# Second FFN of a two-layer trunk: the fourth unit product split in two, its first half ahead of the norm of half 1

## The chip, the cores and the metric

The kernel runs on one core of a Trainium2 chip (trn2). TensorE (PE) multiplies, VectorE (DVE), ScalarE (ACT) and GpSimd (POOL) do the elementwise work, SyncE (SP) issues the transfers. The metric is the device time of one execution in microseconds (us). The kernel before takes 2104.82 us, the median of 3 runs (2103.49 to 2105.01).

## The reference

A trunk of two layers over 1024 latent tokens of 1024 channels with a context of 256 tokens. Layer 0 mixes with a bidirectional gated recurrence, layer 1 with 2-D window means. Each layer then has a gated convolutional feed-forward part (FFN), which is what the change touches in layer 1:

```python
def _conv_ffn(h, w_up, conv_w, conv_b, w_down):
    z = h @ w_up.astype(h.dtype)
    u, v = z[..., :D_FF], z[..., D_FF:]          # D_FF = 3072
    u = _dwconv(u, conv_w, conv_b, (FFN_CONV // 2, FFN_CONV // 2))   # width 3, over positions
    return (jax.nn.gelu(u) * v) @ w_down.astype(h.dtype)

    # in each layer, mod(h) = h * (1 + scale) + shift
    x = x + g_m * _rms_norm(y_lat, norm_post_mix[i])
    f_lat = _conv_ffn(_modulate(_rms_norm(x, norm_pre_ffn[i]), sh_f, sc_f), ...)
    x = x + g_f * _rms_norm(f_lat, norm_post_ffn[i])
```

All data are float32. The kernel gets near-float32 products out of three passes in a rounded type: each operand is split into a rounded part (`_hi`) and the remainder (`_lo`), and a product is hi x hi + hi x lo + lo x hi.

## The kernel before, in words

**Layout.** Channels lie on the 128 partitions in 8 tiles (k = 0 to 7), positions along the free axis in two halves of 512, half 0 and half 1 (`hs(h)`). `H_hi` and `H_lo` hold the normed and modulated input of the FFN. A weight tile of 128x1024 comes by DMA into a raw buffer (`rawA`, `rawB`, `rawC`), ACT rounds it into `W?_hi`, POOL subtracts and writes `W?_lo`.

**The FFN** goes in steps j = 0 to 23 of 128 hidden channels. Steps 0 and 1 compute their u and v directly, and each is a "unit product": 8 tiles k x 3 passes x 2 halves = 48 matmuls of 512 columns. Slot A makes u of step 0, slot B makes v of step 0, slot C (`extra`) makes u of step 1, and slot A a second time makes v of step 1; this is the fourth unit product. From step 2 on the up projection is made by a block scheme of seven quarter products (names 11, 12, S1 to S4, 22) from sums of weight blocks that POOL forms (`combine`) in `So_raw` and in `rawB`; ACT rounds these into `So_hi`, POOL writes the remainder into `So_lo`. `So_lo` and `So_raw` are one and the same memory. After each step `down` multiplies the gated product (`F_hi`, `F_lo`) with the down weights (`WC_hi`, `WC_lo`) into 8 output tiles; in step 0 ACT copies these out of PSUM (`copy_down`), in later steps DVE adds them.

**Ahead of the second FFN.** `first_pair(L, h)` is the function that runs the unit products on half h. On half 0 of layer 1 it runs A and B by turns, then C. Then comes the norm of half 1 (`norm(6, 1)`): three groups of column sums of squares (`square_sums`, 4 matmuls of 1 column each, shown as x8 in the trace), the root on ACT, the reciprocal on DVE, and `spread`, which lays the result over the partitions by four small matmuls. Then `first_pair(1, 1)` on half 1, then the fourth product on both halves, then `down(1, 0)` and the first block step.

**What sets the order.** Each engine has its program in the order in which it is written, and semaphores tie them together. Names that matter here: `w_ready["A"]` says that a slot's weight is split; `unit_done["A"]` that a product of slot A is through; `made` that a block sum stands; `d_copied` that ACT has emptied a tile of `down`. POOL's program at the start of the second FFN (`ffn_first`) is `WA_lo` for the fourth product, block sums S1 and S2 (`So_raw`), `F_lo` of step 0, `WC_lo` of step 0, block sums S3 and S4, and then remainders for the first block step. ACT makes the rounded halves of S4 and S1 ahead of its first `copy_down`, and `down` stops ahead of its fourth tile until that copy is done.

Of the kernel before, what the change touches and what calls it, by code (L numbers as in the profile page):

```python
# [19 lines left out]
P = 128  # L20
# [54 lines left out]
def build_trunk(nc, xT, ctxT, params, ada, wA, wB, wC, gatew, poolw, poolcnt, ident_in, outT):  # L75
    with ExitStack() as top:
# [101 lines left out]
        def nth(order, name, t):  # L178

            return len(order) * t + (order.index(name) + 1 - len(order))  # L180
# [3 lines left out]

        def ready_at(name, t, first=False):
            return nth(READY_FIRST if first else READY_ORDER, name, t)

        def unit_at(s, L, j=0):

# [153 lines left out]
        def evens_to(q, h):  # L343
            each = {"tree": 3, "late": 2, "acc": 0, "pool": 0}
            return sum(chain_end(n, h) - 1 if form(n, h) == "chain" else each[form(n, h)] for n in range(q))
# [236 lines left out]
        def _(pe):  # L582
# [60 lines left out]
                if last:  # L643
                    mm.then_inc(ssq_done[h], 1)

            def square_sums(q, h):

                last, total = square_slot(q, h, KT - 1), square_slot(q, h, 0)
                kind = form(q, h)
                if kind == "chain":  # L650
                    end = chain_end(q, h)
                    if q % 2 == 0:
                        for p in range(end, KT):
                            pe.wait_ge(sq_made[h], 8 * q + p + 1)
                            column_sums(q, h, *square_slot(q, h, p), p == end, False)
                    pe.wait_ge(sum_even[h], evens_to(q + 1, h))
                    column_sums(q, h, *total, q == 1 or end == KT, q != 1 or end == KT)
                    if q == 1 and end < KT:
                        pe.wait_ge(sq_made[h], 8 * q + KT)
                        column_sums(q, h, *last, False, True)  # L660
                elif kind == "late":
                    for n in range(4):
                        if n < 2:
                            pe.wait_ge((sum_even, sum_odd)[n][h], (evens_to, odds_to)[n](q + 1, h))
                        else:
                            pe.wait_ge(sq_made[h], 8 * q + n + 5)
                        column_sums(q, h, *square_slot(q, h, n if n < 2 else n + 4), n == 0, n == 3)
                elif kind == "pool":
                    pe.wait_ge(sum_odd[h], odds_to(q + 1, h))
                    column_sums(q, h, *total, True, True)  # L670
                elif kind == "tree":
                    pe.wait_ge(sum_last[h], trees_to(q + 1, h))
                    column_sums(q, h, *total, True, True)
                else:
                    pe.wait_ge(acc_copied, 1)
                    column_sums(q, h, *total, True, True)
# [270 lines left out]

            def first_pair(L, h):

                a, b, c = ("A", AB01), ("B", AB45), ("C", AB23)  # L950
                joint = 6 if h else 0 if L == 0 else KT
                order = [(u, k) for k in range(joint) for u in (a, b)]
                order += [(u, k) for u in (a, b) for k in range(joint, KT)]
                order += [(c, k) for k in range(KT)]
                for (s, banks), k in order:
                    if k == 0 and s == "C":
                        pe.wait_ge(extra_ready, L + 2)
                        if L == 0:
                            pe.wait_ge(y_evac, 2 * KT)
                    elif k == 0:  # L960
                        pe.wait_ge(w_ready[s], unit_at(s, L) + 1)
                    wait_h(pe, 2 + 2 * L, h, k)
                    if (L, h, s) == (0, 0, "A"):
                        if k == 0:
                            pe.wait_ge(y_evac, KT + 5)
                        if k == 3:
                            square_sums(1, 1)
                        if k == 7:
                            spread(1, 1)
                    if (L, h, s, k) == (1, 0, "A", 4):  # L970
                        square_sums(5, 1)
                    if (L, h, s, k) == (1, 0, "A", 7):
                        spread(5, 1)
                    mm = product(s, k * P, [piece(banks, H_hi, H_lo, k, h)], k == 0, k == KT - 1)
                    if h == 1 and k == KT - 1:
                        mm.then_inc(extra_done if s == "C" else unit_done[s], 1)

            def ffn(L):

                first_pair(L, 0)  # L980
                if L == 0:
                    pe.wait_ge(cols_full, 16)
                    pe.matmul(ps[:, 6, 8:8 + 4 * KT], cnt_row[0:4 * KT], ident[0:4 * KT, 0:4 * KT],
                              start=True, stop=True).then_inc(cols_made, 1)
                    ada_columns(4 * NH + 2, 2, ps[:, 6, 0:2])
                norm(2 + 4 * L, 1)
                first_pair(L, 1)

                pe.wait_ge(w_ready["A"], unit_at("A", L, 1) + 1)
                if L == 0:  # L990
                    pe.wait_ge(ada_added, NH + 2)
                for k in range(KT):
                    mm = product("A", k * P, [piece(AB67, H_hi, H_lo, k, h) for h in range(2)], k == 0, k == KT - 1)
                mm.then_inc(unit_done["A"], 1)
                if L == 0:
                    pe.wait_ge(u_evac, 2)
                    ada_direct(ps[:, 3, 0:2])
                down(L, 0)
                ffn_step(L, 2)
                with pe.Fori(3, FJ - 1) as j:  # L1000
                    ffn_step(L, j)
                ffn_step(L, FJ - 1)
                down_last(L)
# [85 lines left out]
        def _(act):  # L1089
# [191 lines left out]
            def round_second(L):  # L1281

                act.wait_ge(raw_full["A"], 16 * raw_at("A", L, 1) + 16)
                act.wait_ge(unit_done["A"], unit_at("A", L) + 1)
                A(W_hi["A"][:], raw["A"][:], ACT.Copy).then_inc(w_hi["A"], 1)

            for m in range(KT):
                act.wait_ge(out0_done, m + 1)
# [84 lines left out]

            def ffn_first(L):

                round_second(L)
                copy_u(L, 0, AB01)
                round_t(L, 0)
                gelu(L, 0)
                round_t(L, 2)  # L1380
                round_f(L, 0)
                round_down(L, 0)
                copy_u(L, 1, AB23)
                round_t(L, 1)
                if L == 0:
                    act.wait_ge(ada_out, NH + 3)
                for name in ("S4", "S1"):
                    round_op(name, L, 2)
                act.wait_ge(t_raw, 16 * L + 12)
                copy_down(L, 0)  # L1390
                copy_down(L, 1)
                for name in ("11", "12"):
                    round_op(name, L, 2)
                for m in range(2, 6):
                    if m == 4:
                        act.wait_ge(t_raw, 16 * (L + 1))
                    copy_down(L, m)
                round_op("S2", L, 2)
                copy_down(L, 6)
                gelu(L, 1)  # L1400
                copy_down(L, 7)
                act.wait_ge(unit_done["A"], unit_at("A", L, 1) + 1)
                round_t(L, 3)
                for name in ("S3", "22"):
                    round_op(name, L, 2)
# [103 lines left out]
            fill_ffn(1, 0, range(5))  # L1509
            norm_root(5, 1)  # L1510
            fill_ffn(1, 0, range(5, KT))
            squares_x(6, 2, 1, range(KT))
            norm_root(6, 1)
            fill_ffn(1, 1)
# [3 lines left out]
        def _(pool):  # L1518
# [170 lines left out]

            def ffn_first(L):  # L1690

                lo_of_unit("A", unit_at("A", L, 1))
                combine("S1", L, 2)
                combine("S2", L, 2)
                f_remainder(L, 0)
                lo_of_unit("C", DN * L)
                combine("S3", L, 2)
                combine("S4", L, 2)
                for name in READY_FIRST[:5]:
                    lo_of_op(name, L, 2)  # L1700
                for k in range(KT // 2):
                    pool.wait_ge(t_hi, 16 * L + 12 + k + 1)
                    TT(T_lo[3][:, k], T_raw[3][k], T_hi[3][:, k].bitcast(F32), ALU.subtract)\
                        .then_inc(t4_lo, 1)
                for name in READY_FIRST[5:]:
                    lo_of_op(name, L, 2)
# [93 lines left out]
            odd_sum(5, 1, 5)  # L1800
            lo_of_extra(1)
            fill_ffn(1, 0)
            add_odd(2, 1, (1, 3, 5, 7))
            fill_ffn(1, 1)
            ffn(1)
# [602 lines left out]
```

## Time and profile before

| | us |
|---|---|
| median of 3 runs | 2104.82 (2103.49 to 2105.01) |
| the profiled execution, whole | 2108.7 |
| its span, first to last instruction | 2106.9 |
| PE busy / DVE busy / POOL busy / ACT busy | 2025.1 / 1517.2 / 1295.8 / 843.0 |
| mean granted TensorE clock | 0.976 of full speed |

The profiled execution took 2108.7 us, of which 2106.9 are the span that its trace covers; 1.8 us lie around it. Busy times overlap between engines. A busy PE is not a PE at its peak, since matmuls are pipelined: a matmul of 512 columns is shown with 390 ns, but in an unbroken stream one starts every 0.227 us. How much the whole waits for PE is read from its gaps, and where a gap stands the row names the instruction that ended it.

### The profile page before, as it was taken

The numbers are of one execution on the slowest core, as the hardware profiler recorded it, in microseconds if no ns is written. First come the engines' busy times: TensorE is split into PE (matmuls) and PEld (weight loads), VectorE is DVE, ScalarE is ACT, GpSimd is POOL, SyncE is SP. The second block draws the span as 40 slices with busy tenths as digits, with TensorE's granted clock in tenths as the row PEclk, the third lists the DMA queues.
The fourth block names the chain that finished last, engine by engine and source line by source line (L and its number), as shares of the span: only waits on it lengthen the run. The fifth ranks groups of instructions, "written<-read, shape, count | busy, mean of one in ns | idle before, by whom it ended". The sixth has DMA issues, their size and how long they took to land.

```text
span 2106.9 us, 26627 instructions
## 1 busy us (share of the span) xinstructions
PE 2025.1 (96%) x9048; PEld 1662.4 (79%) x9048; DVE 1517.2 (72%) x1510; ACT 843.0 (40%) x1119; POOL 1295.8 (62%) x836
## 2 busy tenths in 40 slices
PE   6899999999999999999999999799999999999996
PEld 6677776877778888888888768688888888888885
DVE  7588888978677777777777774697656665676557
ACT  4576768446322323232322355473332233222322
POOL 4534244655877877877787462368766676667653
PEclk9999999998999999999999988799999999999998
DMA  7132322531222222222222400211111111111114
GB/s 310 65 115 80 114 80 90 200 141 34 97 90 89 80 90 90 77 88 94 90 70 90 170 31 11 90 51 70 40 50 60 60 43 50 57 60 50 50 40 160
DMA packets 55931, 179.68 MB, mean 85 GB/s; under 512 B 5040, under 2 KB 6352, under 8 KB 55248
## 3 DMA queue, kind: packets, MB, share of 16 engines
q1 hardware_dynamic: 55888, 179.13, 23.8%
q8 instruction: 25, 0.41, 0.1%
q14 instruction: 18, 0.15, 0.0%
HBM read 166.52 MB, written 12.58 MB: 85 GB/s over the span
## 4 chain that ended last, share of the span: by engine, by line
PE 79%; DVE 7%; ACT 7%; issue 3%; POOL 3%; DMA 1%; ACTq 0%; POOLq 0%; SPq 0%; DVEq 0%
PE ps L908 38%; PE ps L587 32%; PE ps L755 3%; PE ps L1023 1%; PE ps L641 1%; PE ps L1060 1%; DVE ps L1979 1%; ACT TH L1237 1%; PE ps L689 1%; DVE sq L1838 1%; DVE Y L1918 1%; DMA ada_first<-ada 1%; ACT RA L1240 1%; ACT TH L1247 1%; ACT L1247 0%
## 5 line engine op out<-in xcount | busy, mean ns | idle before, releaser
L2100 DVE TENSOR_TENSOR Y<-Y,ps 128x1024 f32<-128x1024 f32 x336 | 406.0, 1219 | 35.6 <-PE ps L587 0.2
L1710 POOL TENSOR_TENSOR F_lo<-S,F_hi 128x1024 fp32r<-128x1024 f32 x44 | 107.0, 2431 | 328.4 <-ACT F_hi L1372 328.4
L587 PE MATMUL ps<-F_hi,WC_hi 128*128 128x512 f32 x736 | 231.8, 393 | 4.1 <-DVE Y L2100 1.6
L1124 ACT ACTIVATE So_hi<-So_raw 128x512 fp32r<-128x512 f32 x132 | 82.6, 627 | 374.3 <-POOL So_raw L1585 370.2
L587 PE MATMUL ps<-F_hi,WC_lo 128*128 128x512 f32 x736 | 230.0, 390 | 0.0
L1347 ACT ACTIVATE S<-S 128x1024 f32<-128x1024 f32 x48 | 51.0, 1062 | 442.1 <-DVE S L2204 442.0
L587 PE MATMUL ps<-F_lo,WC_hi 128*128 128x512 f32 x704 | 217.5, 390 | 0.0
L1688 POOL TENSOR_TENSOR So_lo<-So_raw,So_hi 128x512 fp32r<-128x512 f32 x132 | 187.5, 1447 | 6.1 <-ACT So_hi L1124 6.1
L587 PEld LDWEIGHTS ps<-F_hi,WC_hi 128*128 128x128 f32 x736 | 138.4, 189 | 34.8 <-DVE Y L2100 2.4
L587 PEld LDWEIGHTS ps<-F_hi,WC_lo 128*128 128x128 f32 x736 | 138.7, 188 | 29.1
L587 PEld LDWEIGHTS ps<-F_lo,WC_hi 128*128 128x128 f32 x704 | 132.7, 189 | 27.8
L1524 POOL TENSOR_TENSOR WA_lo<-rawA,WA_hi 128x1024 fp32r<-128x1024 f32 x20 | 57.6, 2880 | 154.2 <-DVE u L2008 113.3
L1860 DVE TENSOR_REDUCE red<-E 128x128 f32<-128x1024 f32 x45 | 90.9, 2020 | 71.8 <-POOL E L1557 71.8
L2261 DVE TENSOR_TENSOR U<-t,ps 128x512 f32<-128x512 f32 x44 | 30.2, 687 | 153.2 <-PE ps L908 153.2
L908 PE MATMUL ps<-H_hi,WA_hi 128*128 128x512 f32 x352 | 136.9, 389 | 0.0
L908 PE MATMUL ps<-H_lo,WA_hi 128*128 128x512 f32 x352 | 136.9, 389 | 0.0
L908 PE MATMUL ps<-H_hi,WA_lo 128*128 128x512 f32 x352 | 136.9, 389 | 0.0
L908 PE MATMUL ps<-T_hi,So_hi 128*128 128x512 f32 x352 | 136.9, 389 | 0.0
L908 PE MATMUL ps<-T_lo,So_hi 128*128 128x512 f32 x352 | 136.9, 389 | 0.0
L908 PE MATMUL ps<-T_hi,So_lo 128*128 128x512 f32 x352 | 136.9, 389 | 0.0
L1688 POOL TENSOR_TENSOR WA_lo<-rawA,WA_hi 128x512 fp32r<-128x512 f32 x88 | 114.8, 1325 | 2.8 <-ACT WA_hi L1124 2.8
L1688 POOL TENSOR_TENSOR WB_lo<-rawB,WB_hi 128x512 fp32r<-128x512 f32 x88 | 114.6, 1325 | 0.0
(302 smaller groups left out, 5379.8 us busy)
## 6 DMA issues: line engine op xcount, KB each, us to landing
rawA<-wA SPq DMA_DIRECT2D x62, 512.0 KB, 3.2
rawB<-wB SPq DMA_DIRECT2D x62, 512.0 KB, 3.2
E<-ada SPq DMA_DIRECT2D x46, 512.0 KB, 3.2
rawC<-wC SPq DMA_DIRECT2D x46, 512.0 KB, 3.6
quad<-ada SPq DMA_DIRECT2D x8, 2048.0 KB, 9.1
ada_first<-ada SPq DMA_DIRECT2D x4, 2048.0 KB, 15.6
outT<-X SPq DMA_DIRECT2D x16, 512.0 KB, 3.6
X<-outT SPq DMA_DIRECT2D x16, 512.0 KB, 7.1
```

The source lines that it names most:

```text
L587: mm = pe.matmul(out, w[:, w_cols:w_cols + P], (hi, lo)[part], start=first and w is W_hi[s] and part == 0, stop=last and w is W_lo[s])
L641: mm = pe.matmul(ps[:, ssq_bank(q, h), 4 * h + t:4 * h + t + 1], src[:, at + t * P:at + t * P + P], ones[:, 0:1], start=first and t == 0, ...
L755: mm = pe.matmul(out, gw[:, gi], src, start=True, stop=True)
L908: mm = pe.matmul(ps[:, (OUT_FIRST if first else OUT)[name]], w[:, at + k * P:at + k * P + P], right[part][:, k], start=k == 0 and w is hi ...
L1124: A(dst[:, at:at + HF], src[:, src_at:src_at + HF], ACT.Copy).then_inc(op_hi, 1)
L1347: A(S[0][:], S[0][:], ACT.Gelu_apprx_tanh).then_inc(gelu_done, 1)
L1524: TT(W_lo[s][:], raw[s][:], W_hi[s][:].bitcast(F32), ALU.subtract).then_inc(w_ready[s], 1)
L1688: TT(lo[:, at:at + HF], src, hi[:, at:at + HF].bitcast(F32), ALU.subtract).then_inc(op_ready, 1)
L1710: TT(dst[:], S[1][:], F_hi[:].bitcast(F32), ALU.subtract).then_inc(f_ready, 1)
L1860: dve.tensor_reduce(red[:, i], src[:].rearrange("p k m -> p m k"), mybir.AxisListType.X, ALU.add)\
L2100: TT(Y[:, m], Y[:, m], flat(ps[:, b:b + 2, :]), ALU.add).then_inc(d_added, 1)
L2261: TT(U2[:], t1[:], p["S2"], ALU.add).then_inc(up_added, 1)
```

## The change

In layer 1 alone, the fourth unit product is cut into its two halves and becomes slot "D" of `first_pair`. Half 0 (24 matmuls) runs right behind C on half 0, ahead of the norm of half 1, and the first group of that norm's column sums is put ahead of its tile k = 4. Half 1 (24 matmuls) stays where the product was, behind C on half 1. Since slot A's buffers `WA_hi` and `WA_lo` are in use until half 1 is through, the weight of D is split into the first 1024 columns of `So_hi` and `So_lo`. ACT rounds it ahead of the squares of half 1, and POOL takes the remainder ahead of its part of `X`. As the block sums of POOL are written to the memory of `So_lo`, POOL now waits for the whole of D (`unit_done["A"]`) ahead of block sum S1. Layer 0 is as before.

```diff
@@ names
+        W_hi["D"], W_lo["D"] = So_hi, So_lo
@@ square_sums: a chain's sums in two calls
-            def square_sums(q, h):
+            def square_sums(q, h, early=None):
...
-                        for p in range(end, KT):
+                        for p in range(end, KT) if early is None else (end,) if early else range(end + 1, KT):
...
+                    if early:
+                        return
@@ first_pair, PE
-                order += [(c, k) for k in range(KT)]
+                order += [(u, k) for u in ((c, d) if L else (c,)) for k in range(KT)]
...
+                    elif k == 0 and s == "D":
+                        pe.wait_ge(w_ready["A"], unit_at("A", L, 1) + 1)
...
+                    if s == "D" and h == 0 and k == 4:
+                        square_sums(6, 1, early=True)
...
-                        mm.then_inc(extra_done if s == "C" else unit_done[s], 1)
+                        mm.then_inc(extra_done if s == "C" else unit_done["A" if s == "D" else s], 1)
@@ round_second, ACT; now called behind fill_ffn(1, 0), no more at the head of ffn_first(1)
+                if L:
+                    act.wait_ge(ssq_done[0], 7)
+                    A(So_hi[:, 0:D], raw["A"][:], ACT.Copy).then_inc(w_hi["A"], 1)
@@ ffn_first, POOL
-                lo_of_unit("A", unit_at("A", L, 1))
+                if L:
+                    pool.wait_ge(unit_done["A"], unit_at("A", L, 1) + 1)
+                else:
+                    lo_of_unit("A", unit_at("A", L, 1))
                 combine("S1", L, 2)
                 combine("S2", L, 2)
                 f_remainder(L, 0)
@@ POOL, behind fill_ffn(1, 0)
+            pool.wait_ge(w_hi["A"], unit_at("A", 1, 1) + 1)
+            TT(So_lo[:, 0:D], raw["A"][:], So_hi[:, 0:D].bitcast(F32), ALU.subtract).then_inc(w_ready["A"], 1)
             add_odd(2, 1, (1, 3, 5, 7))
```

PE at the norm of half 1, before. `ones,S` and `ones,V` are the column sums, `ident,rstd` the spread, `WC` the last of C on half 0 and `WA` the first on half 1.

```order
1784 L587 MATMUL ps<-H_hi,WC_lo 128x512
1785 L641 MATMUL ps<-ones,S 128x1 [waits sq_made1]
1786 L641 MATMUL ps<-ones,S 128x1 x3
1787 L641 MATMUL ps<-ones,S 128x1 [waits sq_made1]
1788 L641 MATMUL ps<-ones,S 128x1 x3
1789 L641 MATMUL ps<-ones,V 128x1 [waits sum_even1]
1790 L641 MATMUL ps<-ones,V 128x1 x3
1791 L689 MATMUL ps<-ident,rstd 128x128 [waits rstd_made1]
1792 L689 MATMUL ps<-ident,rstd 128x128 x3
1793 L587 MATMUL ps<-H_hi,WA_hi 128x512 [waits h_ready_even,w_ready_A]
```

And now, the same place; `So` is the weight of D.

```order
1784 L589 MATMUL ps<-H_hi,WC_lo 128x512
1785 L589 MATMUL ps<-H_hi,So_hi 128x512 [waits h_ready_even,w_ready_A]
...
1796 L589 MATMUL ps<-H_hi,So_lo 128x512
1797 L643 MATMUL ps<-ones,S 128x1 [waits sq_made1]
1798 L643 MATMUL ps<-ones,S 128x1 x3
1799 L589 MATMUL ps<-H_hi,So_hi 128x512 [waits h_ready_even]
...
1810 L589 MATMUL ps<-H_hi,So_lo 128x512
1811 L643 MATMUL ps<-ones,S 128x1 [waits sq_made1]
1812 L643 MATMUL ps<-ones,S 128x1 x3
1813 L643 MATMUL ps<-ones,V 128x1 [waits sum_even1]
1815 L693 MATMUL ps<-ident,rstd 128x128 [waits rstd_made1]
```

Twelve matmuls of D stand ahead of the first column sums and twelve behind them.

POOL from the remainders of half 0 to the block sums, before.

```order
199 L1535 TENSOR_TENSOR H_lo<-Y,H_hi 128x512 [waits h_hi] x4
200 L1567 TENSOR_TENSOR X<-X,Y 128x512 [waits y_scaled] x4
201 L1535 TENSOR_TENSOR H_lo<-Y,H_hi 128x512 [waits h_hi] x4
202 L1524 TENSOR_TENSOR WA_lo<-rawA,WA_hi 128x1024 [waits w_hi_A]
203 L1585 TENSOR_TENSOR So_raw<-rawB 128x512 [waits op_done,raw_full_A,raw_full_B]
204 L1585 TENSOR_TENSOR So_raw<-So_raw,rawA 128x512 [waits op_done,combined]
205 L1710 TENSOR_TENSOR F_lo<-S,F_hi 128x1024 [waits f_hi]
206 L1524 TENSOR_TENSOR WC_lo<-rawC,WC_hi 128x1024 [waits w_hi_C]
```

And now.

```order
199 L1552 TENSOR_TENSOR H_lo<-Y,H_hi 128x512 [waits h_hi] x4
200 L1824 TENSOR_TENSOR So_lo<-rawA,So_hi 128x1024 [waits w_hi_A]
201 L1584 TENSOR_TENSOR X<-X,Y 128x512 [waits y_scaled] x4
202 L1552 TENSOR_TENSOR H_lo<-Y,H_hi 128x512 [waits h_hi] x4
203 L1602 TENSOR_TENSOR So_raw<-rawB 128x512 [waits raw_full_A,op_done,raw_full_B,unit_done_A]
204 L1602 TENSOR_TENSOR So_raw<-So_raw,rawA 128x512 [waits op_done,combined]
205 L1730 TENSOR_TENSOR F_lo<-S,F_hi 128x1024 [waits f_hi]
206 L1541 TENSOR_TENSOR WC_lo<-rawC,WC_hi 128x1024 [waits w_hi_C]
```

The remainder of the fourth product's weight moved from position 202 to position 200, and the first block sum got a wait for `unit_done_A`; `F_lo` and `WC_lo` stand behind it as they did.

## Rows read from the trace of the kernel before

**Rows 1.** Busy time by stretch: stretch, length, busy per engine, clock, DMA share, GB/s
```profile
1358.00:1373.00 15.00, 10.60 (x41) 9.35 (x42) 9.76 (x14) 5.82 (x11) 3.59 (x3) 0.54 0.17 65
...
1800.00:2000.00 200.00, 200.00 (x884) 165.60 (x883) 123.75 (x120) 60.30 (x84) 131.06 (x87) 1.00 0.15 50
```
**Rows 2.** Timeline of PE, end of C on half 0 to first product on half 1
```profile
1356.17 0.39 PE L587 MATMUL ps<-H_hi,WC_lo 128*128 128x512 f32 x1
1358.31 1.14 PE L641 MATMUL ps<-ones,S 128*128 128x1 f32 x8 [1.75 <-ACT S L1143]
...
1362.31 1.87 PE L641 MATMUL ps<-ones,V 128*128 128x1 f32 x8 [0.41 <-DVE V L1838]
1364.74 2.08 PE L689 MATMUL ps<-ident,rstd 128*128 128x128 f32 x8 [0.57 <-DVE rstd L1852]
1369.36 0.77 PE L587 MATMUL ps<-H_hi,WA_hi 128*128 128x512 f32 x1 [2.54 <-DVE H_lo L1911]
```
**Rows 3.** Timeline of PE, column sums at full clock; matmuls at either clock
```profile
1341.90 0.95 PE L641 MATMUL ps<-ones,V 128*128 128x1 f32 x8
1342.71 0.49 PE L587 MATMUL ps<-H_hi,WA_hi 128*128 128x512 f32 x1
...
1371.20 0.63 PE L587 MATMUL ps<-H_lo,WB_hi 128*128 128x512 f32 x1
1371.63 0.63 PE L587 MATMUL ps<-H_hi,WB_lo 128*128 128x512 f32 x1
...
1373.09 0.39 PE L587 MATMUL ps<-H_hi,WB_hi 128*128 128x512 f32 x1
```
**Rows 4.** Timeline of PE: fourth product, down of step 0, first block step, down of step 1
```profile
1387.40 0.62 PE L587 MATMUL ps<-H_hi,WA_hi 128*128 128x512 f32 x2
...
1398.28 0.62 PE L587 MATMUL ps<-F_hi,WC_hi 128*128 128x512 f32 x2
...
1403.27 0.73 PE L587 MATMUL ps<-F_hi,WC_hi 128*128 128x512 f32 x2 [0.75 <-ACT Y L1410]
...
1410.35 0.39 PE L908 MATMUL ps<-H_hi,WA_hi 128*128 128x512 f32 x1
...
1430.00 0.74 PE L587 MATMUL ps<-F_hi,WC_hi 128*128 128x512 f32 x2 [0.20 <-POOL WC_lo L1524]
```
**Rows 5.** Timeline of POOL at the start of the second FFN
```profile
1381.99 2.41 POOL L1524 TENSOR_TENSOR WA_lo<-rawA,WA_hi 128x1024 fp32r<-128x1024 f32 x1 [3.97 <-ACT WA_hi L1285]
1389.08 1.31 POOL L1585 TENSOR_TENSOR So_raw<-rawB 128x512 f32<-128x512 f32 x1 [4.68 <-DMA rawB<-wB]
1390.47 1.63 POOL L1585 TENSOR_TENSOR So_raw<-So_raw,rawA 128x512 f32<-128x512 f32 x1
1392.06 2.86 POOL L1710 TENSOR_TENSOR F_lo<-S,F_hi 128x1024 fp32r<-128x1024 f32 x1
1394.88 2.84 POOL L1524 TENSOR_TENSOR WC_lo<-rawC,WC_hi 128x1024 fp32r<-128x1024 f32 x1
1397.69 1.74 POOL L1585 TENSOR_TENSOR rawB<-rawA,rawB 128x512 f32<-128x512 f32 x1
1399.38 1.74 POOL L1585 TENSOR_TENSOR So_raw<-rawA,So_raw 128x512 f32<-128x512 f32 x1
```
**Rows 6.** Timeline of ACT: WC_hi, and rounded block sums ahead of the first copy
```profile
1391.50 1.04 ACT L1105 ACTIVATE WC_hi<-rawC 128x1024 fp32r<-128x1024 f32 x1
...
1401.16 1.16 ACT L1124 ACTIVATE So_hi<-So_raw 128x512 fp32r<-128x512 f32 x2 [2.21 <-POOL So_raw L1585]
```
**Rows 7.** Timeline of POOL, where D's weight is now split, and a remainder without contention
```profile
1346.39 1.30 POOL L1535 TENSOR_TENSOR H_lo<-Y,H_hi 128x512 fp32r<-128x512 f32 x1 [0.62 <-ACT H_hi L1160]
1351.32 1.68 POOL L1567 TENSOR_TENSOR X<-X,Y 128x512 f32<-128x512 f32 x1 [3.63 <-DVE Y L1918]
```
**Rows 8.** Timeline of DVE: alone, and beside POOL's F_lo
```profile
1380.37 0.68 DVE L2158 TENSOR_TENSOR T_raw<-Y 128x512 f32<-128x512 f32 x1
...
1392.57 2.90 DVE L2178 SCALAR_TENSOR_TENSOR T_raw<-Y,M,T_raw 128x512 f32<-128x512 f32 x1
```

More of the change, by code:

```diff
@@ L948, in first_pair @@
             def first_pair(L, h):
-                a, b, c = ("A", AB01), ("B", AB45), ("C", AB23)
+                a, b, c, d = ("A", AB01), ("B", AB45), ("C", AB23), ("D", AB67)
                 joint = 6 if h else 0 if L == 0 else KT
@@ L985, in ffn @@
                     ada_columns(4 * NH + 2, 2, ps[:, 6, 0:2])
-                norm(2 + 4 * L, 1)
+                if L == 0:
+                    norm(2, 1)
+                else:
+                    square_sums(6, 1, early=False)
+                    spread(6, 1)
                 first_pair(L, 1)
-                pe.wait_ge(w_ready["A"], unit_at("A", L, 1) + 1)
                 if L == 0:
+                    pe.wait_ge(w_ready["A"], unit_at("A", L, 1) + 1)
                     pe.wait_ge(ada_added, NH + 2)
[L992 to L995, printed above, removed]
+                    for k in range(KT):
+                        mm = product("A", k * P, [piece(AB67, H_hi, H_lo, k, h) for h in range(2)],
+                                     k == 0, k == KT - 1)
+                    mm.then_inc(unit_done["A"], 1)
                     pe.wait_ge(u_evac, 2)
@@ L1283, in round_second @@
                 act.wait_ge(raw_full["A"], 16 * raw_at("A", L, 1) + 16)
-                act.wait_ge(unit_done["A"], unit_at("A", L) + 1)
-                A(W_hi["A"][:], raw["A"][:], ACT.Copy).then_inc(w_hi["A"], 1)
+                if L:
+                    act.wait_ge(ssq_done[0], 7)
+                    A(So_hi[:, 0:D], raw["A"][:], ACT.Copy).then_inc(w_hi["A"], 1)
+                else:
+                    act.wait_ge(unit_done["A"], unit_at("A", L) + 1)
+                    A(W_hi["A"][:], raw["A"][:], ACT.Copy).then_inc(w_hi["A"], 1)
             for m in range(KT):
@@ L1374, in ffn_first @@
             def ffn_first(L):
-                round_second(L)
+                if L == 0:
+                    round_second(L)
                 copy_u(L, 0, AB01)
@@ L1511, in _ @@
             fill_ffn(1, 0, range(5, KT))
+            round_second(1)
             squares_x(6, 2, 1, range(KT))
@@ L1690, in ffn_first @@
             def ffn_first(L):
-                lo_of_unit("A", unit_at("A", L, 1))
+                if L:
+                    pool.wait_ge(unit_done["A"], unit_at("A", L, 1) + 1)
+                else:
+                    lo_of_unit("A", unit_at("A", L, 1))
                 combine("S1", L, 2)
```

## The prediction

> **What bounds the kernel now.** I read the busy time by stretch first, then the gaps of PE. In the loop of the second FFN, PE is busy in 200.00 of 200 us at clock 1.00 [rows 1]: from the first loop step on, PE alone sets the time, and a delay ahead of the loop comes out at the end undiminished. The start of this FFN is different. In the stretch 1358 to 1373 PE is busy for 10.60 of 15 us, and the granted clock is 0.54, so it is mostly at the lower of its two levels, 1.2 in place of 2.4 GHz [rows 1]. The timeline shows why: C on half 0 issues its last matmul at 1356.17, and until 1369.36 there are only the short matmuls of the norm, with gaps ended by ACT's squares, DVE's sums and reciprocal and at last DVE's `H_lo` [rows 2]. This hole of some 13 us is what the change fills.
>
> The second thing to see is the hand-over from the fourth product to `down`. The fourth product starts at 1387.40 and `down` at 1398.28 without a gap [rows 4]. But `WC_lo`, which `down` needs, is POOL's, and POOL is through with it at 1397.69 [rows 5], a mere 0.6 us ahead. POOL came to it by S1, S2, `F_lo` and `WC_lo` in this order, from 1389.08 on. So two engines arrive nearly together, and what PE gains alone is worth at most 0.6 us.
>
> **Step 1: PE on half 0.** 24 matmuls go into the hole. 48 take 1398.28 - 1387.40 = 10.88 us, so one takes 0.227 and 24 take 5.44 [rows 4]. D starts at 1356.40 (1356.17 + 0.227). Twelve run to 1359.12, the first column sums cost 1342.71 - 1341.90 = 0.81 at full clock [rows 3], twelve more run to 1362.65. The other two groups of sums follow: to 1363.46 and 1364.27, with a tail of 0.14 (0.95 - 0.81) 1364.41. Before, the last sums ended at 1362.31 + 1.87 = 1364.18 [rows 2], so they are 0.2 late, and the root and reciprocal too. The spread is then won back: it took 2.08 at the low clock; at the full one, by the ratio of the sums (0.95 to 1.87), it takes 1.06. The first product on half 1 comes at 1369.36 + 0.2 - 1.0 = 1368.6, 0.8 earlier.
>
> **Step 2: how much of that arrives at D on half 1.** PE now idles or does tiny matmuls from 1362.65 to 1368.6, 5.9 us, about as long as the stretch that had brought the clock down before: C ended at 1356.40, the sums at 1358.31 still took 1.14 us, those at 1362.31 took 1.87 [rows 2]. I take it that the clock falls again and comes back at about the same moment, 1373.0, where the rows go from 0.43 apart to 0.39 us each [rows 3]. Then 0.8 us more at the low clock is 1.9 matmuls, or 0.4 us at full clock. Bounds: if the clock stays up, the nine low-clock matmuls of the start (1369.36 to 1373.09, 0.2 us too long each, 1.8 in all) are mostly won, less a wait for the second `H_lo`, so 2.0 earlier in all; if it has fallen before the spread, 0.3 later. D on half 1 then ends at 1387.40 - 0.4 + 5.44 = **1392.4** (1390.8 to 1393.1). Here PE is 5.9 us ahead of before.
>
> **Step 3: what is late next.** `F_lo` and `WC_lo` are ready to be made: `WC_hi` stood at 1391.50 + 1.04 = 1392.5 before [rows 6], and ACT has lost the 1.06 us of rounding ahead of it and starts 0.4 earlier, so some 1391.1; it is bounded by the load of `rawC`, which hangs on C's end. But POOL is not free. Its first block sum now waits for all of D, and queued behind that wait in its program are S1, S2, `F_lo`, `WC_lo`, S3, S4 and all remainders of the first block step. `down` on PE waits for the fourth of them, ACT's rounding for the sixth. Before, S1 began at 1389.08, when `rawB` landed [rows 5]; that load is now 24 us earlier (its buffer is free once POOL has split D's weight) and no longer matters. From the start of S1 to the end of `WC_lo` POOL took 1397.69 - 1389.08 = 8.61 us beside a busy DVE [rows 5]. Bounds: all four at their contended price, 2 x 1.69 + 2.82 + 2.81 = 9.0 (starts apart, rows 5); all four undisturbed, 2 x 1.30 + 2 x 2.41 = 7.4 [rows 5, 7]. DVE has as much to do as before, so I take 8.6. `WC_lo` is through at 1392.4 + 0.05 + 8.6 = **1401.1**, and PE, idle for 8.7 us from 1392.4, starts `down` there: 2.8 us later than before.
>
> The Trainium skill ("SBUF — State Buffer", section "SBUF: two separate sides") says that POOL and a DVE operation with two SBUF inputs lock one port pair for a whole instruction, and the loser blocks fully. The trace agrees in kind: a DVE operation of 0.68 takes 2.90 beside `F_lo` [rows 8]. By that rule alone each POOL operation would wait for a DVE one: 2 x (1.30 + 0.68) + 2 x (2.41 + 0.68) = 10.1, an estimate, 1.5 above the rows; the sum goes by the rows.
>
> **Step 4: the clock at `down`.** After 8.7 us idle the clock will be low. As at 1369.36, nine matmuls go at 0.427, and then 0.227. The first three tiles are 18 matmuls: 9 x 0.427 + 9 x 0.227 + 0.14 = 6.0, so the fourth tile at 1407.1. The other bound on it, ACT's copy, was 1403.27 - 1397.69 = 5.58 behind `WC_lo` (S3 and S4 on POOL, two roundings, the copy) [rows 4 to 6]: 1406.7, hidden by the first. Before, the fourth tile stood at 1403.27. The delay is **3.8**. From there on the spacing is as before: the first block step at 1410.35 + 3.8, `down` of step 1 at 1429.8 + 3.8. Before it started at 1430.00, having waited 0.20 for `WC_lo` [rows 4]; POOL's part there hangs on the end of `down`, with over 3 us of room now, since DVE is ahead. So **+3.6** goes into the loop.
>
> **At no cost.** ACT's rounding (1.06, as any 128x1024 copy) lies between the last `H_hi` of half 0 and its first square, and POOL's remainder (2.41) between 1347.69 and 1351.32 [rows 7], starting 0.2 behind ACT at some 1347.6: it ends at 1350.1, 1.2 ahead of the need. If that cover went, the norm of half 1 would be late by what is over. `rawA` for it landed long before. The weight load of PE overlaps as now.
>
> **The sum.** -0.8 (spread) reduced to -0.4, -5.44 (half of D), then +0.05 + 8.6 for POOL against a `down` at 1398.28, +1.0 for the low clock against 1403.27 - 1398.28, -0.2: +3.6. Against its own execution 2108.7 + 3.6 = 2112.3; that execution is 3.9 above the median, and by the same difference the median becomes 2104.82 + 3.6 = **2108.4 us**. Range of the forecast itself: +1.5 to +4.2.
>
> **Rivals.** (a) *Half the price.* The clock stays up over the norm (D ends at 1390.8) and POOL runs undisturbed (7.4): `WC_lo` at 1398.3, the fourth tile by the low clock at 1404.3, +0.8, 2105.6. For it: the clock fell before after a gap of 1.9 us with nothing on PE at all (1356.40 to 1358.31), and now the sums follow the products at once. Against: DVE is busy beside POOL. 0.20, with a bit on either side of before.
> (b) *PE's gain stands, faster.* If POOL did not hold `down`, half of D would be gone from the path: -5.44, 2099.4. It decides whether `F_lo` and `WC_lo` stand at 1392.4. Against it is POOL's order, in which both come behind the wait. 0.07, for what I have misread in that queue.
> (c) *Heavier.* POOL fully contended (9.0), D's end at 1393.1, and eleven matmuls at the low clock: `WC_lo` at 1402.2, the fourth tile 1408.6, +5.1, 2109.9. The port rule of the Trainium skill ("SBUF — State Buffer", "SBUF: two separate sides") would come out here as well, at an estimated 1.5 above the forecast. 0.31.
> (d) *The change doesn't do what it says*: D's weight comes late on POOL, the squares of half 1 shift, PE stalls before the norm. +0.5 on top at most, 0.02.
> The forecast has 0.40.
>
> **Chances and range.** A measurement of this kernel tells about 0.2% from no change, 4.2 us: 2100.6 and 2109.0. Faster: 0.07, by (b). Same: the forecast, (a) and (d), 0.62. Slower: (c), 0.31. The range runs from 2104.6, just under (a), to 2110.8, just over (c).
>
> **What would show it.** In the profile after: 24 matmuls of `H, So` from about 1356.4; the spread near 1 us long; the last matmul of D near 1392; right behind it POOL's `So_raw<-rawB`, idle before it for over 10 us with PE named; a PE gap of 8 to 9 us ahead of the first `F_hi, WC_hi`, released by POOL's `WC_lo`; spacings of 0.43 in `down`; then no gap at `down` of step 1. I am wrong if that gap is under 5 us, if POOL's S1 starts ahead of D's end, or if `down` runs at full clock and DVE leaves POOL alone, which would bring the two times together.

## The result

| | us |
|---|---|
| before, median of 8 runs | 2104.16 (2101.01 to 2108.26) |
| changed, median of 8 runs | 2109.43 (2107.48 to 2115.05) |
| ratio, 95% interval | 1.0032 (1.0022 to 1.0042) |
| the same two, timed again | 1.0015 (1.0004 to 1.0026) |
| and a third time | 1.0021 (1.0011 to 1.0032) |

By the first ratio the change costs 6.7 us (the two medians differ by 5.3), by the next two 3.2 and 4.4, in the mean of the three 4.8. The forecast was +3.6 and "no change that can be told"; slower by over 0.2% had 0.31. The measured median lies inside the range of 2104.6 to 2110.8, but all three intervals lie above 1: the kernel is slower.

The whole spans of the two profiled executions hide this: 2106.9 before, 2106.5 after. The reason lies ahead of the change, where the granted clock differs from execution to execution (from 1200 to 1340 us it was 0.84 in the profile before, 0.87 in the one after and 0.89 in a second one of the kernel before): C on half 0 ends at 1356.40 before [rows 2] and at 1351.30 after. So all stretches below are counted from that end, and I call the times **marks**:

| from the end of C on half 0, us | before | before, 2nd profile | after | after, 2nd | after, 3rd |
|---|---|---|---|---|---|
| first product on half 1 | 12.96 | 12.96 | 12.49 | 12.49 | 12.49 |
| D (fourth product) ends | 41.88 | 42.14 | 36.47 | 36.43 | 36.58 |
| `WC_lo` ends | 41.32 | 42.82 | 45.79 | 45.76 | 45.90 |
| `down` of step 0 starts | 41.88 | 42.88 | 45.84 | 45.82 | 45.95 |
| first block step | 53.95 | 55.46 | 59.31 | 59.29 | 59.44 |
| `down` of step 1 | 73.60 | 74.50 | 78.35 | 78.33 | 78.48 |
| end of the span | 750.50 | 750.98 | 755.20 | 755.26 | 755.23 |

The end of D is counted as the start of its last matmul plus the spacing of 0.227. By the marks the loss is 4.2 to 4.8 us at the end, and 3.8 to 4.9 at `down` of step 1. They repeat within 0.15 us after and within 1.5 before; the end of C ranged over 8.9 us in all the profiles taken (1347.5 in one of the kernel before). Against the first profile before, D ends 5.4 us earlier, and `down` starts 4.0 later: the first is what the change gives, the second what comes of it once POOL's wait is paid.

**The profile after.** Timeline of PE, to be read against [rows 2] and [rows 4] (start, us, engine, line, operation, tiles, idle before and what ended it):

```profile
1357.69 0.95 PE L643 MATMUL ps<-ones,S 128*128 128x1 f32 x8
1358.50 1.03 PE L643 MATMUL ps<-ones,V 128*128 128x1 f32 x8
1360.10 1.16 PE L693 MATMUL ps<-ident,rstd 128*128 128x128 f32 x8 [0.57 <-DVE rstd L1874]
1363.79 0.76 PE L589 MATMUL ps<-H_hi,WA_hi 128*128 128x512 f32 x1 [2.53 <-DVE H_lo L1933]
...
1387.54 0.39 PE L589 MATMUL ps<-H_hi,So_lo 128*128 128x512 f32 x1
1397.14 1.22 PE L589 MATMUL ps<-F_hi,WC_hi 128*128 128x512 f32 x2 [9.21 <-POOL WC_lo L1541]
...
1402.42 0.63 PE L589 MATMUL ps<-F_hi,WC_hi 128*128 128x512 f32 x2
...
1403.81 0.62 PE L589 MATMUL ps<-F_hi,WC_hi 128*128 128x512 f32 x2
...
1410.61 0.39 PE L912 MATMUL ps<-H_hi,WA_hi 128*128 128x512 f32 x1
...
1429.65 0.62 PE L589 MATMUL ps<-F_hi,WC_hi 128*128 128x512 f32 x2
```

The sums and the spread now take 0.95, 1.03 and 1.16 us against 1.87 and 2.08 in [rows 2], that is, at or near full clock. Then, where [rows 4] had no gap, PE stands 9.21 us ahead of `down`, and POOL's `WC_lo` is named. The timeline of POOL, against [rows 5]:

```profile
1388.01 1.91 POOL L1602 TENSOR_TENSOR So_raw<-rawB 128x512 f32<-128x512 f32 x1 [15.55 <-PE ps L589]
1390.00 1.60 POOL L1602 TENSOR_TENSOR So_raw<-So_raw,rawA 128x512 f32<-128x512 f32 x1
1391.56 2.78 POOL L1730 TENSOR_TENSOR F_lo<-S,F_hi 128x1024 fp32r<-128x1024 f32 x1
1394.31 2.78 POOL L1541 TENSOR_TENSOR WC_lo<-rawC,WC_hi 128x1024 fp32r<-128x1024 f32 x1
1397.05 1.72 POOL L1602 TENSOR_TENSOR rawB<-rawA,rawB 128x512 f32<-128x512 f32 x1
1398.74 2.26 POOL L1602 TENSOR_TENSOR So_raw<-rawA,So_raw 128x512 f32<-128x512 f32 x1
```

POOL sat idle for 15.55 us, until D was through. The operands of `F_lo` and `WC_lo` were not ready for all of that time. ACT made them here:

```profile
1384.47 1.05 ACT L1387 ACTIVATE F_hi<-S 128x1024 fp32r<-128x1024 f32 x1
1385.81 1.06 ACT L1116 ACTIVATE WC_hi<-rawC 128x1024 fp32r<-128x1024 f32 x1 [0.29 <-DMA rawC<-wC]
```

`F_hi` stood at 1385.52, 34.2 us from the end of C, and `WC_hi` at 35.6. So the wait of POOL kept S1 and S2 out of the idle time, and it kept back `F_lo`, which was ready 2.2 us before D ended. And the busy time by stretch, against [rows 1] (stretch, length, busy per engine, clock, DMA share, GB/s):

```profile
1357.00:1372.00 15.00, 11.90 (x55) 9.88 (x54) 10.46 (x16) 8.27 (x13) 4.76 (x4) 0.77 0.16 64
...
1388.00:1397.00 9.00, 0.00 (x0) 0.00 (x0) 8.97 (x6) 3.14 (x5) 8.91 (x4) 0.73 0.00 0
1397.00:1403.00 6.00, 5.86 (x15) 4.62 (x16) 5.96 (x4) 1.98 (x4) 5.26 (x4) 0.55 0.00 0
1403.00:1410.60 7.60, 7.60 (x35) 6.28 (x34) 5.88 (x4) 7.33 (x11) 6.16 (x5) 1.00 0.00 0
...
1800.00:2000.00 200.00, 200.00 (x884) 165.60 (x883) 123.78 (x120) 60.68 (x84) 131.82 (x87) 1.00 0.16 51
```

PE does nothing for 9 us, and in the 6 us behind that the granted clock is 0.55, so it is mostly the lower of the two levels: twelve matmuls, from 1397.14 to 1402.42, start about 0.43 us apart. The loop is PE's alone as before, so what is lost ahead of it stays lost. From `down` of step 1 to the end of the span it is 676.4 to 677.0 us in all thirteen profiles, and differences of under 0.6 us at the end of the span say nothing by themselves.

### The profile page after: what moved, and what is told of

Read it like the earlier page. It is cut to its first block, busy times and chain, and to the rows that moved or that the text cites. A ratio compares the mean times of both kernels' runs of the same rounds, so it can differ in the third digit from the quotient of the medians.

```text
span 2106.5 us, 26630 instructions
## 1 busy us (share of the span) xinstructions
PE 2019.3 (96%) x9048; PEld 1658.6 (79%) x9048; DVE 1513.8 (72%) x1510; ACT 842.9 (40%) x1119; POOL 1295.2 (61%) x836
## 4 chain that ended last, share of the span: by engine, by line
PE 81%; ACT 7%; DVE 6%; issue 3%; POOL 2%; DMA 1%; ACTq 0%; POOLq 0%; SPq 0%; DVEq 0%
PE ps L912 39%; PE ps L589 33%; PE ps L759 3%; PE ps L1034 1%; PE ps L643 1%; PE ps L1071 1%; DVE ps L2001 1%; ACT TH L1248 1%; PE ps L693 1%; DMA ada_first<-ada 1%; ACT RA L1251 1%; DVE sq L1860 1%; ACT TH L1258 1%; ACT L1258 0%; ACT L1251 0%
```

## The experiments

The theory: the split of D gives 5.4 us on PE; POOL's wait for D, with S1, S2, `F_lo` and `WC_lo` queued behind it, takes 9 and more. The rivals: the loss is the low clock's; or it comes from another place, the norm or the loads.

**1. The two kernels again.** No edit.

> The changed kernel once more, timed against the kernel before in interleaved rounds, to size the loss and to see whether the profile's account repeats. Counted from the end of C on half 0, the first profile after has down of step 0 starting at +45.8 us (before +41.9), the first block step at +59.3 (before +54.0) and down of step 1 at +78.4 (before +73.6). Theory (POOL's queue behind the wait for D, plus the low clock that follows): the same marks within 1 us, and a time 4.8 us above before (ratio 1.0023). Rival (something outside this stretch also costs): the marks repeat but the time is 6.7 us or more above before (1.0032).

Ratio 1.0015 (1.0004 to 1.0026), marks within 0.1 us (table above).

> The changed kernel a third time, since its first two ratios to before, 1.0032 and 1.0015, lie further apart than their marks, which agree within 0.1 us. Theory: the marks put it 4.3 to 4.8 us above before (750.5 and 751.0 against 755.2 from the end of C), so the ratio comes out between 1.0015 and 1.0030 with the marks unmoved. Rival: a ratio outside that with the marks unmoved would mean that something ahead of C's end differs between the two kernels.

Ratio 1.0021 (1.0011 to 1.0032), marks again unmoved. With three ratios from 1.0015 to 1.0032 and marks that say 4.2 to 4.8 us (1.0020 to 1.0023), nothing calls for a cost outside the stretch. The first ratio was on the high side of it.

> The kernel before once more, to see whether its marks repeat. Counted from the end of C on half 0: first product on half 1 at +13.0, down at +41.9, first block step at +54.0, down of step 1 at +73.6, end of the span at +750.5. Theory: all within 0.1 us, while the time at which C ends moves by several us with the granted clock ahead of it, so the difference of two whole times holds noise that the marks don't. Rival: the marks themselves move by a microsecond or more from run to run, and the four-fifths agreement so far is luck.

For the kernel before the rival was right. The end of the span repeats within 0.5 us (750.98), but the marks inside do not: `down` starts at 42.88, not 41.88, and the first block step 1.5 later. The timelines of POOL and PE of this second profile show where it comes from:

```profile
1381.20 1.83 POOL L1585 TENSOR_TENSOR So_raw<-rawB 128x512 f32<-128x512 f32 x1 [5.41 <-DMA rawB<-wB]
...
1390.40 0.72 PE L587 MATMUL ps<-F_hi,WC_hi 128*128 128x512 f32 x2 [0.57 <-POOL WC_lo L1524]
```

The kernel before waited 5.41 for `rawB` here, against 4.68 in [rows 5], and S1 then took 1.83 in place of 1.31. From the start of S1 to the end of `WC_lo` POOL took 9.1 us, against 8.6 in [rows 5]. `WC_lo` ended 0.7 us behind D and not 0.6 ahead of it, so PE stood 0.57 ahead of `down` already in the kernel before. The changed kernel doesn't wait for `rawB`; its POOL waits for D.

**2. The wait without the split.** In the kernel before, one line:

```diff
                 lo_of_unit("A", unit_at("A", L, 1))
+                if L:
+                    pool.wait_ge(unit_done["A"], unit_at("A", L, 1) + 1)
                 combine("S1", L, 2)
```

> The kernel before with one edit: POOL waits for the fourth product ahead of block sum S1 (the change's wait without its split). Theory (what is queued behind that wait sets down): D ends at +41.7 from C's end, S1 starts 0.2 behind it, WC_lo ends 9.1 later, down starts at +51.0, the first block step at +64.5, the end of the span at +760.3, that is 9.8 us later than before and 5.1 later than the changed kernel. Rival (POOL's queue is short enough to be caught up): down at +45 or earlier and the end less than 3 us later than before.

There is one execution of this kernel, so it is read by its marks. `down` at 51.41, the first block step at 63.99, the end at 759.42 (forecast 51.0, 64.5 and 760.3): 8.4 to 8.9 us later than before and 4.2 later than the changed kernel. In its timeline PE waits as in the changed one:

```profile
1392.09 0.61 PE L587 MATMUL ps<-H_hi,WA_lo 128*128 128x512 f32 x2
1401.79 0.80 PE L587 MATMUL ps<-F_hi,WC_hi 128*128 128x512 f32 x1 [9.09 <-POOL WC_lo L1524]
```

The two matmuls of the first row end D at 42.16, and POOL's S1 starts at 42.41. So the change is two things of opposite sign: the wait costs 8.4 to 8.9, the split gives 4.2 of it back. The rival that POOL catches up is out.

**3. `F_lo` and `WC_lo` ahead of the wait.** In the changed kernel:

```diff
                 if L:
+                    f_remainder(L, 0)
+                    lo_of_unit("C", DN * L)
                     pool.wait_ge(unit_done["A"], unit_at("A", L, 1) + 1)
+                    combine("S1", L, 2)
+                    combine("S2", L, 2)
                 else:
                     lo_of_unit("A", unit_at("A", L, 1))
-                combine("S1", L, 2)
-                combine("S2", L, 2)
-                f_remainder(L, 0)
-                lo_of_unit("C", DN * L)
+                    combine("S1", L, 2)
+                    combine("S2", L, 2)
+                    f_remainder(L, 0)
+                    lo_of_unit("C", DN * L)
```

> The changed kernel with F_lo and WC_lo of step 0 put ahead of POOL's wait for D, and S1 and S2 behind it. Theory (POOL's order holds down): WC_lo ends about 39.7 us after C's end in place of 45.8, down starts there, but its fourth tile now waits for S1 to S4 on POOL and two roundings and a copy on ACT, at about +48.6; the first block step comes 2.0 to 3.4 us earlier than in the changed kernel, so about 2.5 us faster than it and still 2 us slower than before. Rival (the loss is the low clock alone, or lies elsewhere): within 0.5 us of the changed kernel.

Ratio to before 0.9998 (0.9987 to 1.0009), the end at 751.98: 3.2 faster than the changed kernel and 1.0 to 1.5 behind before by the marks, which the ratio can't tell. `down` started at 40.01 and stopped ahead of its fourth tile:

```profile
1390.23 0.74 PE L589 MATMUL ps<-F_hi,WC_hi 128*128 128x512 f32 x2 [3.42 <-POOL WC_lo L1541]
...
1399.08 0.74 PE L589 MATMUL ps<-F_hi,WC_hi 128*128 128x512 f32 x2 [2.86 <-ACT Y L1426]
```

C ended at 1350.22 here, so the fourth tile stands at 48.86 (forecast 48.6): the next bound is S1 to S4 on POOL, two roundings and ACT's copy. `F_lo` started at 34.27, as soon as `F_hi` stood.

**4. The remainder of D's weight in a memory of its own.** In the changed kernel; POOL's wait is gone because nothing overwrites what D reads, and ACT's rounding into `So_hi` waits instead:

```diff
-        W_hi["D"], W_lo["D"] = So_hi, So_lo
+        D_lo, = overlay(140 + FR, ("D_lo", [P, D], F32R))
+        W_hi["D"], W_lo["D"] = So_hi, D_lo
...
-                if L:
-                    pool.wait_ge(unit_done["A"], unit_at("A", L, 1) + 1)
-                else:
+                if L == 0:
                     lo_of_unit("A", unit_at("A", L, 1))
...
+                if L:
+                    act.wait_ge(unit_done["A"], unit_at("A", L, 1) + 1)
                 for name in ("S4", "S1"):
                     round_op(name, L, 2)
...
-            TT(So_lo[:, 0:D], raw["A"][:], So_hi[:, 0:D].bitcast(F32), ALU.subtract).then_inc(w_ready["A"], 1)
+            TT(D_lo[:], raw["A"][:], So_hi[:, 0:D].bitcast(F32), ALU.subtract).then_inc(w_ready["A"], 1)
```

> The changed kernel with the remainder of D's weight in a memory of its own (the 4 KB that the last layer's E no longer needs), so that POOL's block sums don't overwrite it and POOL doesn't wait for D; ACT's rounding into So_hi waits instead. Theory: POOL makes S1 and S2 before D ends, WC_lo ends at about +39.4 from C's end, down starts there, its fourth tile at +45, the first block step at about +52.3: 5 to 7.5 us faster than the changed kernel and 0 to 2 us faster than before. Rival (the split itself costs, through the squares, the norm or the load of rawB): down starts early but the time stays above before by 2 us or more. Rival (low clock alone): within 1.5 us of the changed kernel.

> The kernel with D's remainder in a memory of its own, again, beside the changed kernel and the next one on one chip. Theory: end of the span at +748.1 from the end of C as before, 7.1 us below the changed kernel and 2.4 to 2.9 below before; ratio to before 0.9984 to 0.9990. Rival: its first ratio, 0.9984, was luck of the chip, and it comes out within 0.0005 of 1.

Ratios to before 0.9984 (0.9974 to 0.9995) and 0.9979 (0.9967 to 0.9990); the end at 748.09 and 748.82, 6.4 to 7.1 us below the changed kernel and 1.7 to 2.9 below before (748.1 was expected of the second; both ratios are clear of 1, so its rival is out). D ends at 36.4 and 36.6 as there, the split is the same; POOL's wait is gone. POOL's timeline in the second profile:

```profile
1374.31 1.73 POOL L1605 TENSOR_TENSOR So_raw<-rawB 128x512 f32<-128x512 f32 x1
1376.12 1.62 POOL L1605 TENSOR_TENSOR So_raw<-So_raw,rawA 128x512 f32<-128x512 f32 x1
1387.60 2.93 POOL L1731 TENSOR_TENSOR F_lo<-S,F_hi 128x1024 fp32r<-128x1024 f32 x1 [9.86 <-ACT F_hi L1388]
1390.49 2.80 POOL L1544 TENSOR_TENSOR WC_lo<-rawC,WC_hi 128x1024 fp32r<-128x1024 f32 x1
```

S1 and S2 are made while PE still works on half 1, and what holds `F_lo` now is `F_hi`. PE still stands 3.42 us ahead of `down`, which starts at 40.0 and 40.2: so of the 5.4 us that the split gives on PE only 1.7 to 2.9 come out. Here POOL's wait is undone in the changed kernel (and ACT has one in its place, ahead of its rounding of S4), and in experiment 2 it alone is added to the kernel before: both say that it is the cost. Norm, squares and the early load of `rawB` are as in the changed kernel, and no cost of theirs shows.

**5. The clock.** In the changed kernel, work for PE while it waits, into a bank that is free there; the result is not touched:

```diff
                     pe.wait_ge(u_evac, 2)
                     ada_direct(ps[:, 3, 0:2])
+                else:
+                    pe.wait_ge(u_evac, 2 * L + 1)
+                    for n in range(36):
+                        pe.matmul(ps[:, 0], W_hi["B"][:, 0:P], H_hi[:, 0, hs(0)], start=True, stop=True)
                 down(L, 0)
```

> The changed kernel with 36 added matmuls of 512 columns (8.2 us at full clock) into a free PSUM bank between D and down, which keep PE at work while it waits for POOL; the output is not touched. Theory (the low clock costs about 1.4 us of the loss): down of step 0 runs at full clock, takes 12.1 us in place of 13.5, and the kernel is 1.4 us faster than the changed one (0.5 to 1.8, since ACT's copy bounds the fourth tile nearly as late). Rival (the clock costs nothing because ACT's copy bounds the fourth tile anyway): 0 to 0.3 us. Rival (the clock is most of the loss): 3 us or more.

The clock stays at full through the wait and through `down`'s first tiles:

```profile
1388.50:1397.70 9.20, 8.06 (x36) 6.35 (x34) 9.16 (x6) 3.05 (x5) 9.12 (x5) 1.00 0.00 0
1397.70:1403.70 6.00, 4.38 (x18) 3.30 (x18) 5.96 (x4) 2.03 (x4) 5.26 (x4) 1.00 0.00 0
```

And yet: the first block step at 59.07 against 59.29 to 59.44, the end at 754.80 against 755.20, ratio 1.0018 (1.0006 to 1.0029). The timeline of PE shows where it went:

```profile
1397.76 0.73 PE L589 MATMUL ps<-F_hi,WC_hi 128*128 128x512 f32 x2 [1.20 <-POOL WC_lo L1545]
...
1403.78 0.73 PE L589 MATMUL ps<-F_hi,WC_hi 128*128 128x512 f32 x2 [1.65 <-ACT Y L1430]
```

The first three tiles take 4.37 us in place of 6.67, so the full clock saves 2.3, and PE then waits 1.65 for ACT's copy. The fourth tile comes at 51.98 in place of 52.51: most of the low clock lay in the shadow of the copy. It cost 0.5 at the fourth tile and 0.2 at the first block step; the 0.4 at the end is within the scatter. The expectation had 1.4, and its first rival, that ACT's copy bounds the fourth tile anyway (0 to 0.3), was nearly right.

**6. The column sums in one piece.** In the changed kernel:

```diff
-                    if s == "D" and h == 0 and k == 4:
-                        square_sums(6, 1, early=True)
...
-                    square_sums(6, 1, early=False)
+                    square_sums(6, 1)
```

> The changed kernel with the column sums in one piece behind D on half 0, where the changed kernel puts their first group between the tiles of D. Theory: the three groups cost PE the same 0.81 us wherever they stand and their inputs are ready by then, so the first product on half 1 stays at +12.5 and the end at +755.2, within 0.2 us. Rival (the early group is what wins time in the norm): the first product on half 1 comes at +13.0 or later and the end moves with it.

First product on half 1 at 12.43, end at 755.27, in one execution. The place of the first group is worth nothing that the marks show.

**7. Further in the same direction.** In the kernel of experiment 4, POOL makes S3 and S4 ahead of `F_lo` too, and ACT makes `gelu`, `F_hi` and `WC_hi` ahead of the roundings of T (both orders for the second FFN alone). The diff is shortened to that FFN; the kernel keeps the old order under `if L == 0`:

```diff
                 combine("S1", L, 2)
                 combine("S2", L, 2)
+                if L:
+                    combine("S3", L, 2)
+                    combine("S4", L, 2)
                 f_remainder(L, 0)
                 lo_of_unit("C", DN * L)
-                combine("S3", L, 2)
-                combine("S4", L, 2)
...
                 copy_u(L, 0, AB01)
-                round_t(L, 0)
                 gelu(L, 0)
-                round_t(L, 2)
                 round_f(L, 0)
                 round_down(L, 0)
+                round_t(L, 0)
+                round_t(L, 2)
```

> The kernel with D's remainder in a memory of its own, and two reorderings in layer 1: POOL makes all four block sums before F_lo, and ACT makes the gelu, F_hi and WC_hi of step 0 ahead of the roundings of T. Theory (what bounds down there is F_hi, then F_lo and WC_lo on POOL; S3 and S4 no longer stand between WC_lo and ACT's first copy): WC_lo ends at +38.5 in place of +39.95, down starts there, the step at +51.0 in place of 52.7, the end at +746.4, 1.7 us faster than that kernel and 4.1 faster than before. Rival (something else turns late, such as the roundings of T that ACT now makes later, or rawB's next load): down starts earlier, but down of step 1 stays at +71.7 or later.

It failed: ratio 1.0005 (0.9993 to 1.0016), `down` at 40.99 in place of the 38.5 expected, the end at 749.07. By the marks it is still 1.4 to 1.9 us faster than before, and up to 1.0 slower than experiment 4. DVE's timeline names it:

```profile
1378.17 1.78 DVE L2201 SCALAR_TENSOR_TENSOR T_raw<-Y,dM 128x512 f32<-128x512 f32 x1
1379.87 1.77 DVE L2190 TENSOR_TENSOR T_raw<-Y 128x512 f32<-128x512 f32 x1
1381.57 1.27 DVE L2230 SCALAR_TENSOR_TENSOR S<-Ub,par,S 128x1024 f32<-128x1024 f32 x1
```

Beside POOL's sums DVE takes 1.77 us for what it does in 0.68 alone [rows 8]. The convolution, the third row, starts at 28.4 from the end of C in place of 26.9 in experiment 4's second profile, and `F_hi` is late with it; `F_lo` then took 3.58 us in place of 2.93. "Something else turns late" was right, though it was neither of the two that I named.

**8. ACT's order alone.** The kernel of experiment 4 with ACT's `round_t(L, 0)` behind `round_f` and `round_t(L, 2)` behind `round_down`, and POOL's order unchanged (the diff is shortened to the second FFN as in 7):

```diff
                 copy_u(L, 0, AB01)
-                round_t(L, 0)
                 gelu(L, 0)
-                round_t(L, 2)
                 round_f(L, 0)
+                round_t(L, 0)
                 round_down(L, 0)
+                round_t(L, 2)
```

> The kernel with D's remainder in a memory of its own and one reordering on ACT alone (gelu and F_hi of step 0 ahead of the roundings of T; POOL's order as there). The last attempt at this moved POOL's S3 and S4 ahead too, and DVE's T operations beside them took 1.77 us in place of 0.69, which made the convolution and F_hi late. Theory: without that, F_hi ends at about +32.7, WC_hi (bound by its load) at +35.5, WC_lo at +38.4, down starts there in place of +40.0, the end at +746.5, 1.6 us faster than the kernel it is made from. Rival (down's fourth tile, bound by S3, S4 and ACT's copy, or DVE's T_lo take its place): down starts early, the step and the end move by less than 0.5 us.

`F_lo` starts at 32.93 in place of 34.3 to 34.4, `down` at 39.37 in place of 40.0 to 40.2, the end is at 747.49: 0.6 to 1.3 us better by the marks (0.7 to 0.8 at `down` of step 1), and a ratio of 0.9979 (0.9969 to 0.9989), which the times can't tell from experiment 4. Of the 1.6 us forecast less than half came at `down`, since `F_lo` took 3.62 us where it had taken 2.93. Its median, 2100.03, is the lowest of all kernels here, 4.5 us (0.21%) below before and 9.2 below the changed kernel timed beside it.

## Why the prediction was right or wrong, point by point

**What bounds the kernel, and the rank of the engines: right.** PE gains, POOL is late next, `down` is held behind S1, S2, `F_lo` and `WC_lo`; the gap of "8 to 9 us", released by `WC_lo`, is there with 9.21. That PE's gain alone is worth "at most 0.6 us" rested on one profile; in the second one POOL came 0.7 us behind PE, and it was worth nothing.

**"No change that can be told" was wrong, and two terms of the sum were mis-sized: POOL's chain in step 3 and the low clock in step 4.** +3.6 against 4.2 to 4.8 by the marks and 4.8 by the mean ratio. The 4.2 us that I had called the limit of what can be told was wrong too: the intervals came out at 0.10 to 0.11% to either side, some 2.2 us, so that +3.6 itself (1.0017) would have been told from no change. Against the marks, in us from the end of C:

| | forecast | after | off by |
|---|---|---|---|
| D ends | 36.0 | 36.47 | +0.5 |
| S1 starts behind it | 0.05 | 0.24 | +0.2 |
| S1 to the end of `WC_lo` | 8.6 | 9.08 | +0.5 |
| `down` starts | 44.7 | 45.84 | +1.1 |
| fourth tile | 50.7 | 52.51 | +1.8 |
| first block step | 57.8 | 59.31 | +1.5 |
| `down` of step 1 | 77.2 | 78.35 | +1.15 |

*Steps 1 and 2* were mis-sized a little: the first product on half 1 came 0.5 us earlier, not 0.8. The clock did fall again, as assumed, and half 1 lost those 0.5 us again at its start, where ten matmuls were 0.43 us or more apart (before it was eight, at 0.38 or more). So D ended 5.4 us earlier, which is its half of 5.44, and not 5.9.

*Step 3 is the one that failed in size first.* I took POOL's 8.6 us from [rows 5], where S1 ran undisturbed (1.31), though I had written that DVE is as busy as before; beside it S1 took 1.91, and the upper bound, 9.0, was the right value. The second profile of the kernel before has 9.1, so that 8.6 was one favourable execution. S1 started 0.24 us behind D's end, not 0.05. Together they are 0.7 us. The port rule that I cited from the Trainium skill ("SBUF — State Buffer", section "SBUF: two separate sides") gives 10.1 as an estimate, 1.0 above the 9.08, where my value was 0.5 below it. I had also read [rows 8] loosely: the 2.90 beside `F_lo` belongs to a SCALAR_TENSOR_TENSOR, which takes 0.74 alone, and not to the operation of 0.68. Contention of this kind decided experiment 7.

*Step 4 had the right two bounds on the fourth tile, and both too short.* By the low clock I had nine matmuls at 0.427 and 6.0 us for three tiles; twelve went at that spacing, and the three tiles took 6.67. By S3, S4, two roundings and ACT's copy I had 5.58 behind `WC_lo`; experiment 5, where only that bound is left, shows about 6.1 (S4 2.27 there, against 1.74 in [rows 5]). The first bound came out later, as forecast, by 0.5 us (forecast 0.4). But the "+1.0 for the low clock" in the sum must not be read as the clock's price, which experiment 5 puts at 0.5 us at the fourth tile and 0.2 at the block step.

*At the other end* the small term had the right sign and was too small. From the first block step to `down` of step 1 the first profile before needed 19.65 and the changed kernel 19.04 (1429.65 - 1410.61), so 0.6 came back, not 0.2. My reason for it, that DVE is ahead, isn't shown: the second profile of the kernel before has 19.04 too, and so have the changed kernel's other two. From the fourth tile to the block step another 0.3 came back (6.80 in place of 7.08): these 30 matmuls ran in an unbroken stream at 0.227.

**At no cost: right.** D on half 0 follows C without a gap, and experiments 4 and 6 confirm that the rounding, POOL's remainder and the sums are hidden.

**The rivals.** (a) fails at its condition, the clock fell. (b) did not come. What it describes, the split without the wait, is experiment 4, and there only 1.7 to 2.9 us of its 5.4 come out against before, because `F_hi` is the next bound. (c) is what came, and I had given it 0.31 against 0.40 for the forecast: it has POOL at 9.0, D's end at 36.7, eleven matmuls at the low clock, `WC_lo` at 45.8 and the fourth tile at 52.2, and the profile has 9.08, 36.47, twelve, 45.79 and 52.51. Its +5.1 is over the 4.2 to 4.8 since more came back behind the fourth tile than the 0.2 it took off. (d) did not come.

**The median of before moved too**, from 2104.82 to 2104.16 with 5 runs more, and single runs range over 7 us. The granted clock goes with it: in the last series of the kernel before, the slowest run (2109.99) has a mean of 0.973 and the fastest (2099.31) one of 0.981. That makes 4 us a matter of two or three series of runs.

## What to carry to other kernels

When work moves ahead on the engine that waits, look at who hands over next and by what margin: here POOL was 0.6 us ahead in one profile and 0.7 behind in another, so the move could win next to nothing unless POOL moved too. Take such a margin, and the price of a contended chain, from more than one profile. A wait that protects a borrowed buffer holds up everything that is queued behind it in that engine's program, needed or not; put what doesn't touch the buffer ahead of it, or borrow a buffer whose next writer comes late. And before a low clock is billed, ask for the next bound behind it.

## What the runs showed of the hardware that I had not expected

- POOL's first operation started 0.24 us behind PE's last matmul, repeatedly (S1 at 36.71, 36.68 and 36.82 against D's end at 36.47, 36.43, 36.58, counted as that matmul's start plus 0.227; in experiment 2 it is 0.24 to 0.25 as well).
- Side by side, DVE and POOL come to the same duration, so the contention looks uneven: DVE's 128x512 operation goes from 0.68 to 1.77 beside POOL's sums, whose own go from 1.30 to 1.73, and to 2.8 beside a 1024-column remainder, which itself goes from 2.41 to 2.8. In the kernel of experiment 8 one `F_lo` took 3.62.
- The granted clock ahead of this stretch differs between executions of one kernel by enough to move its time by several us, while 750 us of program behind it repeat within 0.8 us in every pair of profiles of one kernel.
